# Last feed-forward block of a two-layer trunk: differences of the second weight taken while the first projections still run, low halves of its blocks on VectorE, the seven products in another order, and the low halves of the "up" weights from accumulating DMAs

## What is computed

```python
def conv_glu_ffn(h_norm, w_in, conv_w, conv_b, w_out):
    gate, up = jnp.split(h_norm @ w_in, 2, axis=-1)          # 1024 -> 2 x 2816
    padded = jnp.pad(gate, ((0, 0), (CONV_WIDTH - 1, 0), (0, 0)))
    conv = conv_b
    for t in range(CONV_WIDTH):                              # causal depthwise, width 3
        conv = conv + padded[:, t:t + S, :] * conv_w[t]
    return (jax.nn.silu(conv) * up) @ w_out                  # 2816 -> 1024
...
h = h + conv_glu_ffn(rms_norm(h, norm_ffn[l]), ...)
```

## Time and profile before

| | us |
|---|---|
| median of 3 runs | 1416.52 (1416.09 to 1418.0) |
| the profiled execution's own time | 1415.03 |
| its span, first to last instruction | 1413.3 |
| PE busy in the span | 1388.4 (98%), granted clock 0.998 of full |
| DVE, ACT, POOL busy | 879.0, 648.7, 666.3 |

### The profile page before, as it was taken

How to read it: one execution, slowest core, us unless ns; L and a number is a source line. 1 busy time by engine, 2 the same in 40 slices (tenths; PEclk the granted TensorE clock), 3 DMA queues, 4 the chain that set the end, 5 groups by cost and what they waited for, 6 DMA issues and landing times.

```text
span 1413.3 us, 17598 instructions
## 1 busy us (share of the span) xinstructions
PE 1388.4 (98%) x6797; PEld 1135.6 (80%) x6797; DVE 879.0 (62%) x1249; ACT 648.7 (46%) x1109; POOL 666.3 (47%) x365
## 2 busy tenths in 40 slices
PE   8999999999999999999999999999999999999998
PEld 6888778887788888888888887788777878887886
DVE  4584674665776206663265656836658895888687
ACT  6747583665332212322346555735753333334333
POOL 5645663542444344444346367535344434443542
PEclk9999999999999999999999999999999999999999
DMA  6332012331233233333333210223223602530521
GB/s 175 98 99 64 27 46 75 113 111 50 86 104 105 97 92 104 96 90 98 96 90 103 86 61 16 76 71 109 90 66 91 209 24 60 181 117 1 157 67 59
DMA packets 176305, 125.67 MB, mean 89 GB/s; under 512 B 14657, under 2 KB 152672, under 8 KB 176224
## 3 DMA queue, kind: packets, MB, share of 16 engines
q1 hardware_dynamic: 175664, 124.55, 29.4%
q10 hardware_dynamic: 560, 0.01, 0.0%
HBM read 122.44 MB, written 2.10 MB: 88 GB/s over the span
## 4 chain that ended last, share of the span: by engine, by line
PE 88%; DVE 8%; ACT 1%; issue 1%; DMA 1%; SPq 0%; DVEq 0%; ACTq 0%
PE bank L751 25%; PE bank L755 25%; PE bank L753 25%; PE bank L925 2%; DVE h L1912 1%; PE bank L1054 1%; PE bank L1055 1%; PE bank L1134 1%; PE bank L913 1%; PE bank L1094 1%; DVE w_lo L1919 1%; DMA raw<-in_w_ffn_in 1%; DVE Q L2108 1%; PE bank L1209 1%; DVE h_tok L1886 1%
## 5 line engine op out<-in xcount | busy, mean ns | idle before, releaser
L674 POOL TENSOR_TENSOR w_lo<-raw,w_hi 128x1024 fp32r<-128x1024 f32 (+2 forms) x206 | 495.0, 2408 | 596.0 <-ACT w_hi L1334 594.2
L751 PE MATMUL bank<-x_hi,w_hi 128*128 128x512 f32 x944 | 371.5, 394 | 3.8 <-issue 2.5
L755 PE MATMUL bank<-x_hi,w_lo 128*128 128x512 f32 x944 | 367.6, 389 | 0.0
L753 PE MATMUL bank<-x_lo,w_hi 128*128 128x512 f32 x944 | 367.5, 389 | 0.0
L1334 ACT ACTIVATE w_hi<-raw 128x1024 fp32r<-128x1024 f32 (+2 forms) x205 | 212.9, 1040 | 245.4 <-PE bank L755 236.9
L751 PEld LDWEIGHTS bank<-x_hi,w_hi 128*128 128x128 f32 x944 | 177.3, 188 | 47.2 <-issue 7.8
L753 PEld LDWEIGHTS bank<-x_lo,w_hi 128*128 128x128 f32 x944 | 177.3, 188 | 37.6 <-issue 1.4
L755 PEld LDWEIGHTS bank<-x_hi,w_lo 128*128 128x128 f32 x944 | 177.2, 188 | 36.9
L2226 DVE SCALAR_TENSOR_TENSOR conv<-gate_in,gains_all,conv 128x512 f32<-128x512 f32 x44 | 113.4, 2577 | 1.6
L1685 ACT ACTIVATE conv_silu<-conv 128x512 f32<-128x512 f32 x44 | 27.8, 632 | 176.5 <-DVE conv L2227 176.5
L1867 DVE TENSOR_TENSOR h<-h,bank 128x512 f32<-128x512 f32 x48 | 31.8, 681 | 105.3 <-PE bank L755 105.2
(11 more groups left out here) (341 smaller groups left out, 2484.8 us busy)
## 6 DMA issues: line engine op xcount, KB each, us to landing
raw<-in_w_ffn_in SPq DMA_DIRECT2D x88, 512.0 KB, 3.9
raw<-in_w_in SPq DMA_DIRECT2D x27, 512.0 KB, 3.7
raw<-in_w_ffn_out SPq DMA_DIRECT2D x20, 512.0 KB, 3.6
raw<-in_w_mix_out SPq DMA_DIRECT2D x16, 512.0 KB, 3.8
raw<-in_w_ca_kv SPq DMA_DIRECT2D x32, 256.0 KB, 3.2
raw<-in_w_ca_q SPq DMA_DIRECT2D x8, 512.0 KB, 3.4
raw<-in_w_ca_out SPq DMA_DIRECT2D x8, 512.0 KB, 3.9
raw<-in_w_in SPq DMA_DIRECT2D x12, 256.0 KB, 2.9
```

Source lines behind the costliest of these rows:

```text
L674: pool.tensor_tensor(w_lo[gi % SPLIT][:, c0:n], whole[:, c0:n], w_hi[gi % SPLIT][:, c0:n].bitcast(f32), ALU.subtract).then_inc(S["lo_split ...
L751: pe.matmul(o, ah, bh, start=first, stop=False, skip_group_check=shared_bank)
L753: pe.matmul(o, ah, bl, start=False, stop=False, skip_group_check=shared_bank)
L755: mm = pe.matmul(o, al, bh, start=False, stop=last, skip_group_check=shared_bank)
```

## The change

It has four parts.

1. **Order of the products.** a12·b21, which needs no difference, moves from fourth to second place; s1·t1 goes to fourth. Their banks and places in `OUT_OF` move with them.
2. **Differences ahead of the join.** t1, t2 and t3 are taken at the end of one chunk each (`T_CHUNK`), t4 of slab 0 at the end of the last chunk but one, t4 of slab 1 after product 0. The blocks are loaded at other slabs (`B_LOADS`); t2 gets a buffer of its own, `b_u`, where `up_s` and `act` were, and t4 goes to `b_x`. silu now writes into `conv` in place, and `up_s` is gone.
3. **All low halves of the second weight on DVE** (`out_low`); POOL has none of them.
4. **Low halves of the "up" slabs from DMAs.** For every up slab of the last layer but the first, ACT writes the negated rounded slab to `w_lo` in front of its copy to `w_hi`, and POOL issues a DMA that adds `raw` to it.

Some semaphores are merged elsewhere in the kernel with the same waits. The core of the diff:

```diff
-    PRODUCTS = (("a11", "b11"), ("s1", "t1"), ("s2", "t2"), ("a12", "b21"), ("s3", "t3"), ("s4", "b22"), ("a22", "t4"))
+    PRODUCTS = (("a11", "b11"), ("a12", "b21"), ("s2", "t2"), ("s1", "t1"), ("s3", "t3"), ("s4", "b22"), ("a22", "t4"))
...
+    added = [slab_of(LAST, ("up", g, c)) for g in range(len(LG)) for c in range(g == 0, LG[g])]
+    dma_los = {gi: (j % 2, 16 * (j // 2 + 1)) for j, gi in enumerate(added)}
...
+    B_LOADS = ((("up", 3), ("up", 4), ("up", 2), ("gate", 6)), (("gate", 1), ("up", 1), ("gate", 2), ("gate", 3)))
+    T_CHUNK = ({4: "t1", 5: "t2", 6: "t3"}, {3: "t1", 4: "t2", 5: "t3"}, {2: "t1", 3: "t2", 4: "t3"})
...
-        B_HOME = {"b11": b_x, "b12": b_y, "b22": b_z, "b21": b_v, "t1": b_t, "t2": b_x, "t3": b_y, "t4": b_t}
+        B_HOME = {"b11": b_x, "b12": b_y, "b22": b_z, "b21": b_v, "t1": b_t, "t2": b_u, "t3": b_y, "t4": b_x}
...
@@ SP: when the blocks are loaded, and when a raw buffer may be filled
-                    if g == 0:
+                    if g:
+                        last_use = {"b12": 4, "b22": 5, "b11": 6, "b21": 6}[name]
+                        sp.wait_ge(S["out_lo"], out_los[slab_of(LAST, ("out", g - 1, last_use, pair_slabs(g - 1)[-1][0]))])
+                    elif name == "b21":
                         sp.wait_ge(S["hk_evac"], 2 * NT)
                     else:
-                        sp.wait_ge(S["t_lo"], t_count(g - 1, "t4", pair_slabs(g - 1)[-1][0]))
-                        sp.wait_ge(S["lo_split"], pool_los[slab_of(LAST, ("out", g - 1, 5, pair_slabs(g - 1)[-1][0]))])
+                        sp.wait_ge(S["r_bc_done"], past(LAST, "r_bc_done") + 2)
...
-                            sp.wait_ge(S["lo_split"], pool_los[in_ring[r - RAW]])
+                            before = in_ring[r - RAW]
+                            if before in dma_los:
+                                sp.wait_ge(S["hi_split"], before + 1)
+                                sp.wait_ge(lo_in[dma_los[before][0]], dma_los[before][1])
...
@@ POOL
+                        if gi in dma_los:
+                            pool.wait_ge(S["negated"], added.index(gi) + 1)
+                            pool.dma_start(w_lo[gi % SPLIT][:, 0:n], raw[ring_of[gi] % RAW][:, 0:n], accum_op=ALU.add
+                                           ).then_inc(lo_in[dma_los[gi][0]], 16)
+                            continue
...
@@ ACT
+                            if k in dma_los:
+                                act_.activation(w_lo[k % SPLIT][:, 0:n], whole, ACT.Copy, scale=-1.0).then_inc(S["negated"], 1)
                             act_.activation(w_hi[k % SPLIT][:, 0:n], whole, ACT.Copy).then_inc(S["hi_split"], 1)
...
@@ DVE: the join
                         if c == LG[g] - 1:
-                            t_low(g, 1, 0, pair_slabs(g)[0][1])
+                            for s, nk in pair_slabs(g):
+                                out_low(g, 1, s, nk)
...
+                        for q in range(len(PRODUCTS)):
+                            add_product(g, q)
+                            if q + 2 < len(PRODUCTS):
+                                for s, nk in some:
+                                    out_low(g, q + 2, s, nk)
+                            if q == 0:
+                                for s, nk in some[1:]:
+                                    t_sum(g, "t4", s, nk)
```

## The result

The changed kernel takes 1422.2 us in the median of 6 runs (1420.5 to 1424.23), the kernel before, on the same chip, 1416.44 (1415.41 to 1418.7). The ratio is 1.0038, 95% interval 1.0025 to 1.0051: 0.4% slower, where I had forecast 1408.2 and faster; 1422.2 lies outside my forecast's own range (1405 to 1411) and above the wide one (to 1420) too. The profiled execution took 1421.03 us, with a span of 1419.3.

A forecast was written before the change was run, and what follows sets the result against it. PE bounds the kernel (busy 98%), so only its waits and slow clock at the joins, 10.9 us, can be won. Parts 1 to 3 gain 8.3, up slabs 0: 1416.52 - 8.3 = 1408.2 us; own range 1405 to 1411, wide range 1404.5 to 1420.

The forecast's parts named there:

- Parts 1 to 3 win 8.3 us: Joins of the last feed-forward block: of 10.9 us lost, 2.6 us stay, so the first three parts gain 8.3 us.
- the 1.4 us forecast: First group's join: PE waits 1.1 us for product 1's low half, with 0.27 behind it; bounds 0 and 2.0 us.
- not 3.3: First group's join: DVE takes the last gate 3.3 us late, against about 4.2 before the change.
- Part by part added up: Whole sum: parts 1 to 3 gain 8.3 us at the joins, the up slabs' DMAs (part 4) count 0 us.
- D is 6 to 7 us: Up slabs: D, the time from POOL's issue of an accumulating DMA to its landing, taken as 6 to 7 us.
- hold of the issue by DVE: Up slabs: POOL's DMA descriptors may be held during DVE's two-port mode; step 0.55 us unheld, would not spend the cover.
- Room 8.8 and 9.7 us, cover 2 to 3: Up slabs: time available to the DMA, 8.8 us after odd chunks, 9.7 after even; 2 to 3 us to spare.
- Three of the four loads are spread over earlier chunks: First group: block loads, before issued in a burst at 1105.58, move to earlier chunks; no separate cost was put on this.
- The accumulating DMA is slower than its room: Rival, chance 0.22: D over 8.8 us, PE waits at about every second up slab, 10 times x + 0.27.
- the DMAs bite a little: Rival, chance 0.10: block loads meet added DMAs in the first group, or D just above 8.8; 1414 to 1419 us.
- Its worked example: Slow-DMA rival (chance 0.22), up slabs: D = 9.6 costs 10.7 us; D = 11 costs 25, giving about 1425.
- ACT's copy waiting for `raw`: Sign of being wrong in the changed kernel's profile; it would mean the slow-DMA rival (chance 0.22) holds.

The follow-up runs named there:

- e1: The changed kernel without its accumulating DMAs (POOL writes the up slabs' low halves as before): 1426.06 us, ratio 1.0072 to the kernel before.
- e6: The changed kernel with b11's load one slab later in every group and without the accumulating DMAs: 1417.8 us, ratio 1.0008 to the kernel before.
- e3: The changed kernel with b11's load one slab later in the second and third group: 1413.33 us, ratio 0.9982 to the kernel before.
- e5: The changed kernel with b11's load one slab later in every group, DMAs kept: 1406.61 us, ratio 0.9931 to the kernel before.

## Why the prediction was wrong

- **Parts 1 to 3 win 8.3 us.** They won more, together with part 4: the joins lost 11.8 us by the matmul times and now 0.9. The first join has no wait in place of the 1.4 us forecast, and the third loses 0.8 us, of which 0.55 are a wait, in place of 1.2. In the first join the term was mis-sized: DVE took the last gate slab at 1145.46 with PE done at 1143.1 (product 0 begins at 1148.53, less one slab), 2.4 us late and not 3.3. b21's low half was then written from 1152.66 to 1153.9, and PE came to it at 1154.0.
- **Part by part added up.** I gave all of the joins' gain to parts 1 to 3 and priced part 4 at 0. e1 and e6 show that this gain hangs on the fourth part: with POOL's second subtraction back, two differences take 6.8 us and the joins wait 10.0 us. I had the row for it (a convolution step of 2.77 us in place of 0.75) and put POOL's holds into the sum, but took the POOL operation as removed throughout. The sum was right for the whole change and wrong as a price of its parts.
- **D is 6 to 7 us.** Right as a median, 6.9, but D isn't one number: 4.6 alone, 5.4 to 5.7 at a group's start with one raw slab beside it, 8.8 to 9.4 there with b11 too. The estimates that I had worked out from the Trainium skill's fit (DMA: Bandwidth & Descriptors, Anatomy of one DMA), 3.2 us and, with both reads counted, 4.4, come near to the copy and the adding DMA that travel alone (3.0 and 4.6), and fall short of the medians (5.0 and 6.9). POOL's 21 issues took 0.86 to 1.03 us each, so no hold of the issue by DVE, which I had named against the change, shows.
- **Room 8.8 and 9.7 us, cover 2 to 3: the first step that failed.** I read the room from a chunk in the middle of a group, and in the second and third group it was enough for all of the 12 up slabs behind the first (7 + 5). At a group's start the ring still holds a slab of 2.7 us, and the room is 6.5. One reading of the slab order at the group's edge would have shown it, to 0.4 us: 8.8 less 2.7. By itself it cost nothing: in e3 and e5 the DMAs there land in 5.5 to 5.8 us and no slab waits. It took away the cover that a DMA slowed by its neighbour would have needed.
- **Three of the four loads are spread over earlier chunks, at no cost: the step that gave the loss.** I priced the loads' move only by what it took out of the old burst, not by what each new place stands in front of or beside. b11's new place is 1 MB in the same microsecond as an accumulating DMA, in the two shortest rooms (D there 9.4 and 8.9 us), and in the first group a wait for `r_bc_done` with a raw slab queued behind it, which is issued 9.6 us later than before the change. Moving it by one slab gave 8.9 us and then another 6.7. (In the third group b11 was at this place before the change as well; there the change added the DMA to it.)
- **The rival.** "The accumulating DMA is slower than its room" at 0.22 gave the sign, and "the DMAs bite a little" named the meeting with block loads, but both priced it elsewhere: not every second up slab by a slow D, but three slabs by their places. Its worked example is also mis-added: 25 us on 1408.2 is 1433, not 1425. I had named ACT's copy waiting for `raw` as a sign of being wrong, and it came, if not far beyond what was there: 12.0 us in three waits in the first group, 8.0 in three before the change. My forecast's own number, 1408.2, is near e5's (1406.6), the time of this change without its misplaced load. That is in part luck: the joins gave 10.9 us and not 8.3, and three up slabs of the first group still lose 2.7.

What stays open: the three waits of 0.7 to 0.8 us at up slabs of the first group in e5, where the DMA share is 0.69. The trace has a lead for the last of them, at 1126.95: b21's load carries a wait too, for ACT's last `h_tok`, SP stands in it for 16.2 us, and ACT then waits 4.1 us for the raw slab behind it. Whether the waits go with a load moved further or only with fewer DMAs was not tried.

## What to carry to other kernels

A transfer's room is not one number: read it at the shortest place of the pattern, at group edges, where the slabs are smaller, and not from the steady middle. A load that is moved must be costed at its new place: what waits behind it in its queue, which wait it carries in front of it, and which transfer flies beside it. Where POOL's work goes away, price the change with and without that part; a gain on DVE may belong to it.

## What was not expected of the hardware

A DMA that adds into SBUF holds the DMA engines twice as long for its packets as one that copies the same 512 KB (4.2% to 2.1% of the span in 3024 packets). With nothing beside it, it lands 4.6 us after its issue, the copy 3.0; in the median of this kernel 6.9, the copy 5.0. Issued within a microsecond of 1.5 MB of loads, it took 9.4 us, and 5.7 when the 1 MB of b11 among them came later. And two DVE differences of 2.35 us take 4.55 beside one POOL subtraction and 6.76 beside two.
